# Gate products of a one-hot scatter: one full fp32 product against two fp32r products, with some of the one-hot columns on GpSimd

## The chip, the cores and the metric

The kernel runs on one core of one Trainium2 chip. The metric is the device time of one launch in microseconds (us). Three runs of the kernel before took 2625.31, 2624.11 and 2623.07 us, median 2624.11.

## What is computed

Two layers of a hybrid decoder run over 256 prompt tokens and 8 sample tokens. Each layer has three mixers with a common output projection, and then PEER, a product-key retrieval over 128 x 128 experts of one neuron each. The change is in PEER for the prompt tokens. Cut to what matters, the reference says:

```
q = (h @ wq).reshape(T, PEER_HEADS, 2, PEER_KDIM // 2)
s = einsum('thpc,hpkc->thpk', q, subkeys)
s_top, i_top = top_k(s, 16)                    # per head and side
cand = s_top[:, :, 0, :, None] + s_top[:, :, 1, None, :]
cs, ci = top_k(cand, 16)                       # 16 experts per head
g = softmax(cs)                                # their gates
act = gelu(einsum('td,thkd->thk', h, u[e]))
out = einsum('thk,thkd->td', g * act, v[e])
```

An expert is a pair (a, b) with number 128 a + b. A token uses 8 heads x 16 = 128 of the 16384 experts.

## The kernel before, in words

The kernel does not gather rows of u and v for the prompt tokens. It goes over all 16384 experts in 128 tiles of 128: tile j of `peer_u` is loaded, turned by TensorE (`turn_u`, L982), and multiplied with the normed activations of 256 tokens (`z_of`, L992). ScalarE's gelu of the product lands in G (L1266, L1267), which holds one number for each expert, token and tile. G is then multiplied with the gates, and a second stage of 128 tiles (`y_of`, L1038) multiplies it with `peer_v`.

**The gates** come as a dense 128 x 128 table for each token, made by one product: a one-hot matrix of a's (hotA: row = slot of the token, column = expert number a) times a matrix of b's whose one-hot entries carry the gate (hotB). Their product has for every pair the sum of its gates. The 256 tokens are taken in 64 groups of four (GG = 4). Group g is made in tile j = 64 + g, so this work lies in the second half of the first stage alone, in each of the two layers.

**One tile of the second half** on TensorE, in order: `z_of(j)`, 24 fp32r products with 256 moving columns (three for each of 8 pieces, since h and u are each split in a high fp32r part and the rest); `turn_u(j + 2)`, 8 transposes; `gates(g)`, 4 full fp32 products of 128 x 128 x 128 (L1004). Every full fp32 product is two instructions in the profile, each with its own weight load, so `gates` has 8 a tile and L1004 counts 1024 for 2 layers x 64 groups x 4 products.

`gates(g)` waits for three semaphores: hotA_ready (VectorE, L1824, all four tokens in one instruction of 512 columns), hotB_ready (VectorE, L1827, tokens 0 and 1, one instruction each) and hotC_ready (ScalarE, tokens 2 and 3: Abs of the distance to the index at L1250, then Relu with scale and bias at L1254). hotA and hotB have two buffers each, by g % 2, so the columns for group g + 1 can be written while group g is multiplied.

**The other engines in a tile.** VectorE, in order: multiply the rows of G that already have gates (L1851), the low parts of the turned u tile (`turned_low`, L1816), the one-hot columns (L1824, L1827), and `gate_rows` (L1837, L1839), which waits for the gate product and multiplies it into G. ScalarE: gelu, high parts of the turned tile (L1244), the copy of the rest of the gate product (L1292), its one-hot columns. GpSimd does nothing in this stage. Its queue stands at a wait for e_ready, then one for the last z product, and behind them are the indirect loads of expert rows for the sample tokens. SyncE's queue loads the tiles of u and v and copies state.

A granted clock (PEclk) of 1.00 is TensorE's level of 2.4 GHz, 0.50 that of 1.2 GHz.

## Time and profile before

| | |
|---|---|
| median of three runs | 2624.11 us |
| the profiled execution's own time | 2624.88 us |
| its span, first to last instruction | 2623.3 us |
| mean granted TensorE clock | 0.956 |
| PE busy | 2453.7 us, 94% |
| DVE busy | 1621.5 us, 62% |
| ACT busy | 1299.0 us, 50% |
| POOL busy | 105.6 us, 4% |

The engines are PE (TensorE's products), PEld (its weight loads, which overlap PE), DVE (VectorE), ACT (ScalarE), POOL (GpSimd) and SP (SyncE). Busy time is a union of intervals, so where instructions of one engine overlap in the pipeline, busy time is less than count x mean duration. The pace of a run of products is best read from the starts of the weight loads, since the ends of matmuls are modelled.

### The profile page before, as it was taken

The page shows a single profiled execution, that of the slowest core. Times are in us where ns is not written, and L with a number is a line of the kernel's source. Part 1 is how long each engine was busy: PE and PEld are TensorE (multiplying, and loading weights), DVE is VectorE, ACT ScalarE, POOL GpSimd, SP SyncE. Part 2 cuts the span into 40 slices and gives each one's busy share as a digit, 9 for nine tenths or more (in the row PEclk, how much of TensorE's full clock was granted, in tenths as well). Part 3 has the DMA queues.
Part 4 walks back from the last instruction along what each step waited for, and adds up shares of the span by engine and source line. Part 5 has one row for each costly group of instructions (what it writes and reads, how often), then busy time and mean ns, then how long its engine had stood idle before and what let it go on. Part 6 is the DMA issues. An engine that isn't in the chain of part 4 may idle for free.

```text
span 2623.3 us, 46433 instructions
## 1 busy us (share of the span) xinstructions
PE 2453.7 (94%) x17162; PEld 2100.0 (80%) x17162; DVE 1621.5 (62%) x3830; ACT 1299.0 (50%) x2860; POOL 105.6 (4%) x140
## 2 busy tenths in 40 slices
PE   6987899999999999999889878999999999999997
PEld 3564489999999988778645545799999999887785
DVE  2365247775677777767534641577756777776676
ACT  1342223545766666666413421245457666666664
POOL 2100010000000000000011000100000000000000
PEclk9997899999999999999988968999999999999998
DMA  7431226667555557666473312366665555676663
GB/s 231 147 127 66 81 99 224 241 234 252 192 208 191 209 196 242 219 196 194 127 240 130 116 65 81 114 233 244 246 234 196 199 207 195 204 238 221 196 193 128
DMA packets 143189, 482.43 MB, mean 184 GB/s; under 512 B 25282, under 2 KB 52224, under 8 KB 138862
## 3 DMA queue, kind: packets, MB, share of 16 engines
q1 hardware_dynamic: 132478, 439.11, 49.6%
q0 software_dynamic: 10496, 40.42, 4.4%
q8 instruction: 140, 2.29, 0.3%
q14 instruction: 75, 0.61, 0.1%
HBM read 476.20 MB, written 104.21 MB: 221 GB/s over the span
## 4 chain that ended last, share of the span: by engine, by line
PE 90%; DVE 5%; issue 1%; DMA 1%; ACT 1%; SPq 0%; POOL 0%; DVEq 0%; POOLq 0%; ACTq 0%
PE ps L992 28%; PE ps L1038 26%; PE ps L712 13%; PE ps L982 8%; PE ps L1004 4%; PE ps L703 4%; PE ps L721 1%; DMA region<-in_w_in 1%; PE ps L830 1%; PE ps L968 1%; PE ps L860 1%; PE ps L833 1%; PE ps L846 0%; DMA region<-in_cache_k_rope,pidx 0%; DVE big L1360 0%
## 5 line engine op out<-in xcount | busy, mean ns | idle before, releaser
L992 PE MATMUL ps<-parts_hw,parts_uv 128*128 128x256 f32 x6144 | 801.2, 287 | 9.1 <-DVE parts_uv L1816 9.1
L992 PEld LDWEIGHTS ps<-parts_hw,parts_uv 128*128 128x128 f32 x6144 | 754.8, 192 | 10.2 <-issue 10.0
L1038 PE MATMUL ps<-parts_uv,parts_hw 128*128 128x512 f32 x3072 | 705.5, 392 | 11.6 <-DVE parts_hw L1884 8.2
L1038 PEld LDWEIGHTS ps<-parts_uv,parts_hw 128*128 128x128 f32 x3072 | 579.4, 189 | 139.9 <-issue 15.4
L1880 DVE TENSOR_TENSOR parts_uv<-region,parts_uv 128x512 fp32r<-128x512 f32 x512 | 351.7, 691 | 196.1 <-ACT parts_uv L1303 195.8
L1303 ACT CAST parts_uv<-region 128x512 fp32r<-128x512 f32 x512 | 317.8, 622 | 248.7 <-PE ps L1038 247.5
L1816 DVE TENSOR_TENSOR parts_uv<-ps,parts_uv 128x512 fp32r<-128x512 f32 x512 | 329.5, 686 | 163.7 <-ACT parts_uv L1244 160.2
L1244 ACT CAST parts_uv<-ps 128x512 fp32r<-128x512 f32 x512 | 278.9, 599 | 1.5 <-PE ps L982 1.5
L1267 ACT ACTIVATE big<-ps 128x256 f32<-128x256 f32 (+26 forms) x256 | 129.7, 507 | 279.8 <-PE ps L992 279.8
L982 PE MATMUL ps<-ident,region 128*128 128x128 f32 x2048 | 265.5, 273 | 1.4 <-ACT big L1235 1.4
L712 PE MATMUL ps<-region 128*128 128x264 f32 (+3 forms) x832 | 234.1, 442 | 6.7 <-DMA region<-in_w_in 6.0
L982 PEld LDWEIGHTS ps<-ident,region 128*128 128x128 f32 x2048 | 230.0, 141 | 1.7 <-ACT big L1235 1.7
L712 PEld LDWEIGHTS ps<-region 128*128 128x128 f32 x832 | 159.1, 193 | 74.8 <-issue 34.7
L703 PE MATMUL ps<-ident,big 128*128 128x128 f32 (+2 forms) x518 | 102.8, 332 | 73.0 <-DVE big L1390 57.1
L1308 ACT CAST parts_hw<-big 128x256 fp32r<-128x256 f32 x256 | 168.7, 661 | 0.0
L1884 DVE TENSOR_TENSOR parts_hw<-big,parts_hw 128x256 fp32r<-128x256 f32 x256 | 157.8, 617 | 3.3 <-ACT parts_hw L1308 3.2
L703 PEld LDWEIGHTS ps<-ident,big 128*128 128x128 f32 (+2 forms) x518 | 72.4, 173 | 103.0 <-DVE big L1390 58.1
L1851 DVE TENSOR_TENSOR big<-big 128x4 f32<-128x4 f32 (+62 forms) x126 | 54.6, 434 | 155.1 <-ACT big L1267 155.1
L1004 PE MATMUL ps<-region 128*128 128x128 f32 x1024 | 135.2, 275 | 0.0
L1004 PEld LDWEIGHTS ps<-region 128*128 128x128 f32 x1024 | 124.5, 192 | 0.0
L1266 ACT ACTIVATE big<-ps 128x4 f32<-128x4 f32 (+62 forms) x126 | 34.9, 277 | 156.1 <-PE ps L992 156.1
L1254 ACT ACTIVATE region<-big,region 128x128 f32<-128x128 f32 x256 | 111.2, 483 | 0.0
(273 smaller groups left out, 1937.1 us busy)
## 6 DMA issues: line engine op xcount, KB each, us to landing
region<-in_peer_u SPq DMA_DIRECT2D x256, 512.0 KB, 3.9
region<-in_peer_v SPq DMA_DIRECT2D x256, 512.0 KB, 4.3
out<-in_state_win_k SPq DMA_DIRECT2D x16, 1536.0 KB, 8.9
out<-in_state_win_v SPq DMA_DIRECT2D x16, 1536.0 KB, 8.5
out<-in_state_win_k SPq DMA_DIRECT2D x16, 1534.5 KB, 9.1
out<-in_state_win_v SPq DMA_DIRECT2D x16, 1534.5 KB, 7.4
region<-in_peer_wq SPq DMA_DIRECT2D x8, 2048.0 KB, 8.2
region<-in_w_in SPq DMA_DIRECT2D x6, 1536.0 KB, 7.8
```

The lines of the kernel that those rows point to most:

```text
L703: mm = pe.transpose(o[0:cols, c0:c0 + rows], src, ident[0:rows, 0:rows])
L712: mm = pe.matmul(o[0:n_out, 0:cols], lhs, rhs, start=(i == 0), stop=(i == len(parts) - 1))
L982: mm = pe.transpose(ps[:, 2 * (j % 2) + half, 128 * i:128 * i + 128], rows_t[j % UN][:, 128 * c:128 * c + 128], ident[:, :])
L992: mm = pe.matmul(ps[:, 4 + j % 2, 0:SEQ], uT[j % 2][a][:, 128 * c:128 * c + 128], hp[b][:, c, :], start=(c == 0 and n == 0), stop=(c == KD ...
L1004: mm = pe.matmul(ps[:, 6 + g % 2, 128 * k:128 * k + 128], hotA[g % 2][:, k, :], hotB[g % 2][:, k, :], start=True, stop=True)
L1038: mm = pe.matmul(ps[:, 2 * half + t, :], wp[j % UN][a][:, 128 * t:128 * t + 128], vp[j % 2][b][:, 512 * half:512 * half + 512], start=(j = ...
L1244: act.copy(uT[j % 2][0][:, 512 * half:512 * half + 512], ps[:, 2 * (j % 2) + half, :]).then_inc(uT_high, 1)
L1303: act.copy(vp[j % 2][0][:, h], rows_t[j % UN][:, h]).then_inc(v_high, 1)
L1308: act.copy(wp[j % UN][0], G[:, j // JH, :, j % JH]).then_inc(w_high, 1)
L1816: dve.tensor_tensor(uT[j % 2][1][:, h], ps[:, 2 * (j % 2) + half, :], uT[j % 2][0][:, h], ALU.subtract).then_inc(uT_low, 1)
L1880: dve.tensor_tensor(vp[j % 2][1][:, h], rows_t[j % UN][:, h], vp[j % 2][0][:, h], ALU.subtract).then_inc(v_low, 1)
L1884: dve.tensor_tensor(wp[j % UN][1], G[:, j // JH, :, j % JH], wp[j % UN][0], ALU.subtract).then_inc(w_ready, 1)
```

## The change

- hotA and hotB leave their place in the region tile for a tile of their own, `hot_r`, of type fp32r. hotA keeps two buffers by group. hotB's index is now the part: hotB[0] high, hotB[1] low. It has one buffer for all groups.
- The gates of the 256 tokens are split once per layer, at j = 63: ScalarE writes the high part rounded to fp32r (a copy in the place of the negation that Relu needed), VectorE subtracts to get the rest.
- `gates` has two fp32r products for each token, hotA x hotB[0] and hotA x hotB[1], summed in PSUM, with 128 moving columns each.
- VectorE writes both parts of tokens 0 and 1, four instructions for two. GpSimd writes both parts of tokens 2 and 3, four instructions of the same kind. ScalarE's Abs and Relu go.
- With one buffer, the columns of group g + 1 wait for the product of group g. On VectorE they now come after `gate_rows(g)`.
- GpSimd's loop over the 64 groups stands ahead of the indirect loads in its queue.

The diff, cut to its core:

```diff
@@ -177,8 +177,6 @@
         wslot = [region[:, i * 4096:(i + 1) * 4096] for i in range(2)]
         rows_t = [region[:, 4096 + i * 1024:4096 + (i + 1) * 1024] for i in range(UN)]
-        hotA = [region[:, O_HT + i * 512:O_HT + (i + 1) * 512].rearrange("p (a b) -> p a b", a=GG) for i in range(2)]
-        hotB = [region[:, O_HT + 1024 + i * 512:O_HT + 1024 + (i + 1) * 512].rearrange("p (a b) -> p a b", a=GG) for i in range(2)]
         hB = region[:, O_HT:O_HT + 1024]
         gyS = region[0:NB, O_HT:O_HT + 2048].rearrange("p (g c) -> p g c", g=4)
@@ -186,12 +184,15 @@
 
 
         partA = sb("parts_uv", [P, 4 * 1024], F32R)
-        gap = sb("gap", [P, 4 * 1024 + KD * T])
+        gap = sb("gap", [P, 4 * 1024])
+        hot_r = sb("hot_r", [P, KD * T], F32R)
         partB = sb("parts_hw", [P, 4 * 1024], F32R)
         uT = [[partA[:, (2 * i + p) * 1024:(2 * i + p + 1) * 1024] for p in range(2)] for i in range(2)]
         vp = uT
         hp = [partB[:, i * KD * SEQ:(i + 1) * KD * SEQ].rearrange("p (k t) -> p k t", k=KD) for i in range(2)]
         wp = [[partB[:, (2 * i + p) * SEQ:(2 * i + p + 1) * SEQ] for p in range(2)] for i in range(UN)]
+        hotA = [hot_r[:, i * 512:(i + 1) * 512].rearrange("p (a b) -> p a b", a=GG) for i in range(2)]
+        hotB = [hot_r[:, 1024 + i * 512:1024 + (i + 1) * 512].rearrange("p (a b) -> p a b", a=GG) for i in range(2)]
         G = big[:, 0:BIG].rearrange("p (q t j) -> p q t j", q=2, j=JH)
         at = [0]
 
@@ -298,8 +299,7 @@
         rsel = cut(P)[0:TOPK]
         hsum = cut(2 * PH).rearrange("p (s h) -> p s h", s=2)
         tail = big[:, BIG:BIG + TAIL]
-        nw = tail[:, 0:SEQ]
-        dist = [tail[:, SEQ + i * P:SEQ + (i + 1) * P] for i in range(2)]
+        gate = [tail[:, i * SEQ:(i + 1) * SEQ] for i in range(2)]
         act_t = [tail[:, 528 + i * SEQ:528 + (i + 1) * SEQ] for i in range(2)]
         hS = tail[:, 1040:1104].rearrange("p (k b) -> p k b", k=KD)
 
@@ -372,8 +372,9 @@
         coef_ready = sem("sample_weights_ready")
         hotA_ready = sem("onehot_a_ready")
         hotB_ready = sem("onehot_b_ready")
-        dist_ready = sem("onehot_distance")
-        hotC_ready = sem("onehot_b_by_scalar")
+        gate_high = sem("gates_high")
+        gate_low = sem("gates_low")
+        hotC_ready = sem("onehot_b_by_gpsimd")
         g_prod = sem("gate_product")
         g_moved = sem("gate_moved")
         g_used = sem("gate_product_used")
@@ -674,6 +675,15 @@
                     pool.indirect_dma_start(gath[b % 2], None, A[name].rearrange("l e d -> (l e) d"), row).then_inc(done, 16)
 
                 pool.wait_ge(e_ready, 1)
+                pool.wait_ge(gate_low, 1)
+                for g in range(NGRP):
+                    if g:
+                        pool.wait_ge(g_prod, g)
+                    for k in range(2, GG):
+                        tk = slice(GG * g + k, GG * g + k + 1)
+                        for i in range(2):
+                            e = pool.tensor_scalar(hotB[i][:, k, :], iota[:, :], slotT[:, 1, tk], gate[i][:, tk], ALU.is_equal, ALU.mult)
+                    e.then_inc(hotC_ready, 1)
                 pool.wait_ge(z_prod, NK)
                 for b in range(NB):
                     if b >= 2:
@@ -1001,7 +1011,8 @@
                         pe.wait_ge(g_used, g - 1)
                         pe.wait_ge(g_moved, g - 1)
                     for k in range(GG):
-                        mm = pe.matmul(ps[:, 6 + g % 2, 128 * k:128 * k + 128], hotA[g % 2][:, k, :], hotB[g % 2][:, k, :], start=True, stop=True)
+                        for i in range(2):
+                            mm = pe.matmul(ps[:, 6 + g % 2, 128 * k:128 * k + 128], hotA[g % 2][:, k, :], hotB[i][:, k, :], start=(i == 0), stop=(i == 1))
                     mm.then_inc(g_prod, 1)
 
                 wait_moved(pe, "s", 1, 3)
@@ -1243,17 +1254,6 @@
                         act.wait_ge(turned, 2 * j + half + 1)
                         act.copy(uT[j % 2][0][:, 512 * half:512 * half + 512], ps[:, 2 * (j % 2) + half, :]).then_inc(uT_high, 1)
 
-                def onehots(g):
-                    if g >= 1:
-                        act.wait_ge(hotC_ready, g)
-                    for k in range(2):
-                        act.activation(dist[k], iota[:, :], ACT.Abs, bias=slotT[:, 1, GG * g + 2 + k:GG * g + 3 + k], scale=-1.0).then_inc(dist_ready, 1)
-                    for k in range(2):
-                        tk = slice(GG * g + 2 + k, GG * g + 3 + k)
-                        act.wait_ge(dist_ready, 2 * g + k + 2)
-                        e = act.activation(hotB[g % 2][:, 2 + k, :], dist[k], ACT.Relu, bias=slotT[:, 2, tk], scale=nw[:, tk])
-                    e.then_inc(hotC_ready, 1)
-
                 turned_high(0)
                 turned_high(1)
                 for j in range(NK):
@@ -1284,15 +1284,13 @@
                         act.copy(slotT[:, :, t0:t0 + m], o[:, 0:384].rearrange("p (s c) -> p s c", s=3)[:, :, 0:m]).then_inc(moved_a, 1)
                     if j == JH - 1:
                         wait_moved(act, "slot", 1)
-                        act.activation(nw, slotT[:, 2, 0:SEQ], ACT.Copy, scale=-1.0).then_inc(dist_ready, 1)
+                        act.copy(gate[0].bitcast(F32R), slotT[:, 2, 0:SEQ]).then_inc(gate_high, 1)
                     if j >= JH:
                         g = j - JH
                         act.wait_ge(g_prod, g + 1)
                         if g < NGRP - 1:
                             act.copy(G[:, 1, GG * g:GG * g + GG, g + 1:JH],
                                      ps[:, 6 + g % 2, :].rearrange("p (a b) -> p a b", a=GG)[:, :, JH + g + 1:NK]).then_inc(g_moved, 1)
-                    if JH - 1 <= j < NK - 1:
-                        onehots(j - JH + 1)
 
                 def v_parts(j):
                     act.wait_ge(row_ld[j % UN], 16 * (NK // UN + j // UN + 1))
@@ -1815,16 +1813,19 @@
                         dve.wait_ge(uT_high, 2 * j + half + 1)
                         dve.tensor_tensor(uT[j % 2][1][:, h], ps[:, 2 * (j % 2) + half, :], uT[j % 2][0][:, h], ALU.subtract).then_inc(uT_low, 1)
 
-                def onehots(g):
-                    if g == 0:
-                        wait_moved(dve, "slot", 1)
+                def onehots_a(g):
                     if g >= 2:
                         dve.wait_ge(g_prod, g - 1)
                     ta = slotT[:, 0, GG * g:GG * g + GG].unsqueeze(2).to_broadcast([P, GG, P])
                     dve.tensor_tensor(hotA[g % 2], iota[:, :].unsqueeze(1).to_broadcast([P, GG, P]), ta, ALU.is_equal).then_inc(hotA_ready, 1)
+
+                def onehots_b(g):
+                    if g:
+                        dve.wait_ge(g_prod, g)
                     for k in range(2):
                         tk = slice(GG * g + k, GG * g + k + 1)
-                        e = dve.tensor_scalar(hotB[g % 2][:, k, :], iota[:, :], slotT[:, 1, tk], slotT[:, 2, tk], ALU.is_equal, ALU.mult)
+                        for i in range(2):
+                            e = dve.tensor_scalar(hotB[i][:, k, :], iota[:, :], slotT[:, 1, tk], gate[i][:, tk], ALU.is_equal, ALU.mult)
                     e.then_inc(hotB_ready, 1)
 
                 def gate_rows(g):
@@ -1868,10 +1869,17 @@
                         step(dve.scalar_tensor_tensor(efl[:, :], pr[:, 0, :], float(NK), pr[:, 1, :], ALU.mult, ALU.add))
                         settle()
                         dve.tensor_scalar(eidx[:, :], efl[:, :], eoff[:, 0:1], None, ALU.add).then_inc(e_ready, 1)
+                    if j == JH - 1:
+                        wait_moved(dve, "slot", 1)
+                        dve.wait_ge(gate_high, 1)
+                        dve.tensor_tensor(gate[1], slotT[:, 2, 0:SEQ], gate[0], ALU.subtract).then_inc(gate_low, 1)
+                        dve.wait_ge(gate_low, 1)
                     if JH - 1 <= j < NK - 1:
-                        onehots(j - JH + 1)
+                        onehots_a(j - JH + 1)
                     if j >= JH:
                         gate_rows(j - JH)
+                    if JH - 1 <= j < NK - 1:
+                        onehots_b(j - JH + 1)
 
                 def v_low_part(j):
                     for half in range(2):
```

## Rows read from the trace of the kernel before

**Rows 1.** The page's chain that ended last, by line.

```profile
PE ps L992 28%; PE ps L1038 26%; PE ps L712 13%; PE ps L982 8%; PE ps L1004 4%; PE ps L703 4%; PE ps L721 1%; DMA region<-in_w_in 1%; PE ps L830 1%; PE ps L968 1%; PE ps L860 1%; PE ps L833 1%; PE ps L846 0%; DMA region<-in_cache_k_rope,pidx 0%; DVE big L1360 0%
```

**Rows 2.** Windows: first half, second half, value stage; busy us (instructions), PEclk, DMA share, GB/s.

```profile
400.00:640.00 240.00, 240.00 (x2039) 239.33 (x2038) 164.84 (x403) 106.12 (x201) 0.57 (x1) 0.99 0.69 242
642.00:930.00 288.00, 288.00 (x2489) 288.00 (x2488) 206.78 (x497) 197.04 (x563) 0.00 (x0) 1.00 0.57 198
940.00:1305.00 365.00, 357.87 (x1584) 291.99 (x1584) 257.11 (x415) 230.53 (x385) 13.81 (x14) 0.99 0.62 200
```

**Rows 3.** Timeline, one tile of the second half; start us, us, engine, line.

```profile
816.24 0.97 PEld L1004 LDWEIGHTS ps<-region 128*128 128x128 f32 x8
...
817.13 2.93 PEld L992 LDWEIGHTS ps<-parts_hw,parts_uv 128*128 128x128 f32 x24
...
817.44 0.25 ACT L1292 COPY big<-ps 128x104 f32<-128x104 f32 x1 [0.26 <-PE ps L1004]
...
817.94 0.68 DVE L1824 TENSOR_TENSOR region<-iota,region 128x512 f32<-128x512 f32 x1
818.18 0.87 ACT L1254 ACTIVATE region<-big,region 128x128 f32<-128x128 f32 x2
818.54 0.60 DVE L1827 TENSOR_SCALAR region<-iota,region 128x128 f32<-128x128 f32 x2
819.05 0.41 DVE L1837 TENSOR_TENSOR big<-big,ps 128x256 f32<-128x256 f32 x1
819.38 0.30 DVE L1839 TENSOR_TENSOR big<-big,ps 128x152 f32<-128x152 f32 x1
820.01 0.90 PEld L982 LDWEIGHTS ps<-ident,region 128*128 128x128 f32 x8
...
820.88 0.30 PEld L1004 LDWEIGHTS ps<-region 128*128 128x128 f32 x2
```

**Rows 4.** The page's groups: weight loads; busy us, mean ns of one.

```profile
L992 PEld LDWEIGHTS ps<-parts_hw,parts_uv 128*128 128x128 f32 x6144 | 754.8, 192 | 10.2 <-issue 10.0
...
L1004 PEld LDWEIGHTS ps<-region 128*128 128x128 f32 x1024 | 124.5, 192 | 0.0
```

**Rows 5.** The chain in order of time, value stage; start us, us, what.

```profile
950.32 127.85 PE ps L1038 x564
```

**Rows 6.** Timeline, weight loads of full fp32 products with 64 moving columns.

```profile
169.46 0.30 PEld L811 LDWEIGHTS ps<-big,region 128*128 128x128 f32 x2 [0.61 <-ACT region L1159]
169.68 0.30 PEld L812 LDWEIGHTS ps<-big,region 128*128 128x128 f32 x2
169.90 0.30 PEld L813 LDWEIGHTS ps<-big,region 128*128 128x128 f32 x2
```

**Rows 7.** Windows: the stretch around Rows 6.

```profile
169.20:170.30 1.10, 1.07 (x9) 0.84 (x9) 1.07 (x3) 1.10 (x4) 0.00 (x0) 1.00 0.00 0
```

**Rows 8.** Timeline, a late tile of the same half.

```profile
925.12 0.60 DVE L1827 TENSOR_SCALAR region<-iota,region 128x128 f32<-128x128 f32 x2
925.64 0.42 DVE L1837 TENSOR_TENSOR big<-big,ps 128x256 f32<-128x256 f32 x1
925.97 0.41 DVE L1839 TENSOR_TENSOR big<-big,ps 128x244 f32<-128x244 f32 x1
...
927.44 0.64 PEld L1004 LDWEIGHTS ps<-region 128*128 128x128 f32 x5
```

**Rows 9.** Line 1827 by its source view: duration ns min/median/max.

```profile
L1827 DVE TENSOR_SCALAR region<-iota,region x256: 334/342/365, 643.4 to 2237.4; 128x128 f32<-128x128 f32 x128
```

**Rows 10.** GpSimd's groups by line: busy us, mean ns of one.

```profile
L604 POOL MEMSET ones<- 128x128 f32 x1 | 0.2, 204 | 0.3 <-POOLq L1970 0.3
```

**Rows 11.** Waits of the second half: us in total, times, longest us.

```profile
ACT big L1266 <- PE ps L992: 75.4, 61, 1.3
```

**Rows 12.** Timeline, entry into the second half.

```profile
643.38 0.60 DVE L1827 TENSOR_SCALAR region<-iota,region 128x128 f32<-128x128 f32 x2
...
644.81 0.30 PEld L1004 LDWEIGHTS ps<-region 128*128 128x128 f32 x2
```

## The prediction, made before the changed kernel was run

> **What bounds the kernel.** I read the chain first. L992, the products of the first PEER stage, hold 28% of the span, L1038 26%, the transposes L982 8% and the gate products L1004 4% [rows 1]. L1004 is thus on the path with its whole busy time. The stage table says how: in the second half of the first stage TensorE is busy 288.00 us of 288 at clock 1.00, VectorE 206.78, ScalarE 197.04, GpSimd 0 [rows 2]. Nothing there waits for VectorE or ScalarE; the other way round, ScalarE's gelu waits for the z product 61 times, 75.4 us in all [rows 11]. So any nanosecond on TensorE in a tile is paid 128 times (64 tiles in each of two layers), and anything on another engine costs nothing until it passes the slack that I work out below.
>
> The timeline of one tile gives the paces. Weight loads of the gate products start at 816.24, those of the next z at 817.13: 0.89 us for 8 instructions, 111 ns each. The z loads run to 820.01, 2.88 us for 24, 120.0 ns each. Eight transposes take 0.87 us, and the next gate products start at 820.88, 4.64 us after the last [rows 3].
>
> **TensorE's part.** The change keeps the number of instructions: 4 full fp32 products of two instructions each become 8 fp32r products of one. What counts is the spacing of an fp32r product with 128 moving columns, which this trace does not have; all its fp32r products have 256 or 512. The naive reading is that work halves. Two rows speak against it.
>
> First, streaming need not be the limit. L811 to L813 are full fp32 products with a 128-column weight and only 64 moving columns. Their loads start 0.22 us apart for two instructions, 110 ns each, at clock 1.00 [rows 6, 7]. That is the spacing of the gate products too, though these stream twice the columns. So in both a load of 128 weight columns takes the time. Second, the fp32r load is no shorter than the fp32 one: 192 ns mean on L992 and 192 on L1004 [rows 4]. Every fp32r product has its own load too, 6144 loads on L992 though two of three share their weights, so I count no load as saved.
>
> Then where between the ends? Below: streaming alone. The value stage has 564 products of 512 columns in 127.85 us, 226.7 ns each [rows 5]; against 120.0 for 256 columns that is 106.7 ns for 256 columns, 0.417 a column, and 120.0 - 53.3 = 66.7 ns for 128 columns. Above: each fp32r product as dear as the full fp32 product that it takes the place of, 222 ns. Between them lie 111 (the load, at fp32's spacing) and 120.0 (the load, at fp32r's spacing on L992). I take 120.0, because that row is nearest: same type, same load, and the 13 ns over 106.7 that fp32r shows at 512 columns as at 256 look like a cost of each instruction and not of its columns. The term is 1024 x (120.0 - 111) = **+9.2 us**.
>
> The Trainium skill, page "TensorE: Matmul & The Clock Gate", section "Back-to-back issue gap", states some 81 ns for load and product in a sustained stream with 128 moving columns. By that the term would be 1024 x (81 - 111) = -31 us; no row here shows that pace, and the 110 ns of [rows 6] speak against it.
>
> **VectorE's part.** Two more column writes a tile. The pair at L1827 takes 819.05 - 818.54 = 0.51 us, 0.255 each in a stream and 0.34 alone [rows 3, 9], so +0.51 us a tile on an engine busy 206.78 / 288 x 4.64 = 3.33 us of 4.64. It is hidden, if the chain holds: in the new order hotA ends at 818.54; gate_rows, 819.05 to 819.68 before, takes 0.63 to 819.17; four writes, 3 x 0.255 + 0.34 = 1.11, end at 820.28. The next gate products are due at 820.88: slack 0.60 us. In a late tile gate_rows grows: 925.12 + (926.38 - 925.64) + 1.11 = 926.97 against 927.44, slack 0.47 [rows 8]. Some 0.53 on the mean, and 0.07 more where the tile is longer by 8 x 9 ns. Cost nothing; the cover is z of the next tile, and without it each 0.1 us is worth 12.8 us. That these writes wait for the product of group g adds nothing on VectorE, since gate_rows ahead of them waits for the same.
>
> The fp32r output of hotA and hotB: between nothing and a few per cent of 0.5 us; I take nothing.
>
> **ScalarE's part.** Abs and Relu go, the Relu pair alone 0.87 us from 818.18 [rows 3]. ScalarE only waits more for TensorE: no gain.
>
> **GpSimd's part.** Four column writes a tile, from the release of group g's product (817.44, when ScalarE's copy starts) to 820.88: 3.44 us, so 0.86 for each is the limit. The trace has no such instruction on GpSimd. Below stands its memset of 128 x 128, 204 ns [rows 10]; above, twice VectorE's own 342, some 0.68 us, as an estimate. Both fit alone: cost nothing. Its queue: the loop now stands ahead of the indirect loads, which wait for the last z product anyway, and the loop ends a tile before that: nothing.
>
> **Once per layer.** Before, the first columns were ready at 643.38 + 0.60 = 643.98, and TensorE came at 644.81, slack 0.83 [rows 12]. New on VectorE: a subtraction of 256 columns (0.41, as L1837's), its store and wait (0.1, my estimate) and two writes (0.51), 1.02: 0.2 us late, twice, **+0.4 us**. GpSimd starts at 643.3 and ends 0.82 to 2.7 later, so this could be 2 us more.
>
> **Sum.** 9.2 + 0.4 = 9.6 us onto the profiled execution's 2624.88: **2634.5 us**. That execution stands 0.77 above the median of the runs, well within their own spread.
>
> **Rivals.**
> 1. *Loads keep fp32's spacing.* The 13 ns belong to fp32r's streaming, which is hidden at 128 columns, and 111 ns stay. For: L811 and L1004 agree with each other within 1 ns whatever they stream. Against: both are fp32. Time 2624.88 + 0.4 = 2625.3.
> 2. *Streaming is the limit after all (faster).* 66.7 ns: -1024 x 44.3 = -45.4 us, 2579.9. For: "two fp32r passes for four" is the plain count of work, and a load's record of 192 ns may hold latency that overlaps, as it does on L992, where loads start every 120. Against: the 110 ns of [rows 6]. VectorE would just follow: the tile shrinks by 0.35 us, under its slack. The Trainium skill's 81 ns of the page named above is of this kind, and gives 2594.
> 3. *A short fp32r product is as dear as a full fp32 one.* 222 ns: +1024 x 111 = +113.7, 2739. Nothing in the trace excludes it; nothing in it shows such a jump between 512 and 256 columns either.
> 4. *GpSimd ahead of hotA (slower).* GpSimd's four writes start at 817.44, while VectorE still has 0.50 us of low parts to do. If hotA then has to stand behind all four, it starts 4p - 0.50 late, p being one GpSimd write; after a slack of 0.60 the stall is 4p - 1.10 us a tile, from p = 0.28 on. At p = 0.41, twice the memset, 0.54 x 128 = 69 us: 2704. At 0.68 it would be 207. If only one write stands ahead, it decides from p = 0.60 alone. The Trainium skill, page "SBUF — State Buffer", section "Who interferes with whom", gives a reason for such an order: a VectorE instruction with two SBUF inputs, as hotA (index and slots), and a GpSimd one that reads SBUF block each other for a whole instruction. No run here has shown it, GpSimd being idle in this stage.
>
> **How the numbers follow.** Forecast 0.34, rival 1 0.23, rival 2 with all values between 66.7 and 105 ns 0.20, rival 3 0.12, rival 4 0.11. The range goes from 2576, just under rival 2, to 2668, which holds the smaller half of rival 4; out are rival 3 and the rest of rival 4, 0.18. A measurement can tell 0.2%, some 5 us, from no change. Faster by over that: rival 2, 0.20. Within: rival 1, 0.23. Slower: the forecast with its +9.6 us and rivals 3 and 4, 0.57.
>
> **What would show it.** The gate products' weight loads at 120 ns, 0.96 us for 8, and a tile of 4.70 us; 1024 instructions as before; no waits of TensorE on hotB or hotC beyond the first of each layer; hotA starting as the low parts end. A spacing near 111 makes rival 1 right, near 67 rival 2, near 222 rival 3. If TensorE waits in each tile for the columns, rival 4 is right, and hotA's start and p say how. I am wrong altogether if the time moves outside this half stage.

## The result and the profile after

The changed kernel takes 2656.74 us, median of four runs (2654.54 to 2661.28), against 2624.11 before: a ratio of 1.0126, 95% interval 1.0109 to 1.0144. It is 32.6 us, or 1.3%, slower. The forecast was 2634.5, its range 2576 to 2668.

The groups of the page after that answer to [rows 4], [rows 9] and the idle GpSimd of [rows 2]; columns as there (busy us, mean ns of one, idle before and its releaser):

```profile
L685 POOL TENSOR_SCALAR hot_r<-iota,region,big 128x128 fp32r<-128x128 f32 x512 | 444.7, 879 | 593.7 <-DVE big L1875 414.3
...
L1015 PE MATMUL ps<-hot_r 128*128 128x128 f32 x1024 | 138.3, 278 | 17.3 <-issue 11.5
L1828 DVE TENSOR_SCALAR hot_r<-iota,region,big 128x128 fp32r<-128x128 f32 x512 | 152.8, 368 | 0.0
...
L1015 PEld LDWEIGHTS ps<-hot_r 128*128 128x128 f32 x1024 | 123.9, 191 | 34.0 <-issue 29.8
```

The same stretch as in [rows 2] by windows, a little shorter so that the entry is left out (busy us of PE, PEld, DVE, ACT, POOL, then PEclk, DMA share, GB/s):

```profile
645.00:930.00 285.00, 282.84 (x2364) 277.14 (x2364) 231.56 (x590) 106.06 (x296) 200.34 (x239) 0.99 0.55 193
```

GpSimd, idle before, is busy 200 of 285 us, and one of its writes takes 0.88 us on the mean. TensorE has only 2364 instructions in 285 us, where before it had 2489 in 288: the same work at a slower tile. Its gate products still number 1024, and the mean of their loads is 191 ns against 192.

One tile by the timeline, the answer to [rows 3]:

```profile
815.09 0.97 PEld L1015 LDWEIGHTS ps<-hot_r 128*128 128x128 f32 x8
...
815.98 2.94 PEld L1002 LDWEIGHTS ps<-parts_hw,parts_uv 128*128 128x128 f32 x24
...
816.30 3.43 POOL L685 TENSOR_SCALAR hot_r<-iota,region,big 128x128 fp32r<-128x128 f32 x4 [1.39 <-PE ps L1015]
816.72 0.68 DVE L1820 TENSOR_TENSOR hot_r<-iota,region 128x512 fp32r<-128x512 f32 x1
...
817.86 1.17 DVE L1828 TENSOR_SCALAR hot_r<-iota,region,big 128x128 fp32r<-128x128 f32 x4
818.86 0.90 PEld L992 LDWEIGHTS ps<-ident,region 128*128 128x128 f32 x8
...
819.90 0.97 PEld L1015 LDWEIGHTS ps<-hot_r 128*128 128x128 f32 x8
```

The eight gate loads take 815.98 - 815.09 = 0.89 us, 111 ns each, the old pace to the nanosecond. Then the loop shows. The product's release lets GpSimd start at 816.30, its four writes end at 819.73, and the next gate loads start at 819.90. So a tile is 0.89 + 0.32 to GpSimd's start + 3.43 + 0.17 = 4.81 us against TensorE's own 4.64. VectorE's four writes end at 819.03, well before.

Four writes at 0.79 us, what one takes by itself (a row below has it), would be 3.16 us, and the loop 4.54 us, under TensorE's own tile. It is over it because GpSimd's writes grow beside VectorE. In the first layer hotA (L1820) mostly starts 0.3 to 0.5 us after GpSimd's first write. That first write takes 0.79 us, the second, which runs beside hotA, 0.93 by the median, and the third, beside VectorE's column writes (L1828), 0.88.

In the second layer, and there only from about the 27th group on, the tile is longer still:

```profile
2123.61 0.97 PEld L1015 LDWEIGHTS ps<-hot_r 128*128 128x128 f32 x8 [0.45 <-issue]
...
2124.50 2.94 PEld L1002 LDWEIGHTS ps<-parts_hw,parts_uv 128*128 128x128 f32 x24
...
2124.82 0.68 DVE L1820 TENSOR_TENSOR hot_r<-iota,region 128x512 fp32r<-128x512 f32 x1
2124.82 3.78 POOL L685 TENSOR_SCALAR hot_r<-iota,region,big 128x128 fp32r<-128x128 f32 x4 [1.40 <-PE ps L1015]
...
2127.39 0.90 PEld L992 LDWEIGHTS ps<-ident,region 128*128 128x128 f32 x8
...
2128.79 0.97 PEld L1015 LDWEIGHTS ps<-hot_r 128*128 128x128 f32 x8 [0.50 <-issue]
...
2129.95 0.68 DVE L1820 TENSOR_TENSOR hot_r<-iota,region 128x512 fp32r<-128x512 f32 x1
2130.00 1.29 POOL L685 TENSOR_SCALAR hot_r<-iota,region,big 128x128 fp32r<-128x128 f32 x1 [1.39 <-PE ps L1015]
```

Here hotA (L1820) starts just before GpSimd's first write or with it. That write takes 1.29 us. In the tiles of 4.7 to 4.8 us, where GpSimd starts first, a first write takes 0.79:

```profile
811.59 0.79 POOL L685 TENSOR_SCALAR hot_r<-iota,region,big 128x128 fp32r<-128x128 f32 x1 [1.40 <-PE ps L1015]
```

With the longer first write the four take 3.78, and the tile is 0.89 + 0.32 + 3.78 + 0.19 = 5.18 us. The source views give the spread, GpSimd's write first (ns min/median/max):

```profile
L685 POOL TENSOR_SCALAR hot_r<-iota,region,big x512: 780/828/1348, 643.0 to 2271.5; 128x128 fp32r<-128x128 f32 x171
```

```profile
L1820 DVE TENSOR_TENSOR hot_r<-iota,region x128: 670/682/834, 642.8 to 2267.9; 128x512 fp32r<-128x512 f32 x128
L1828 DVE TENSOR_SCALAR hot_r<-iota,region,big x512: 329/343/454, 643.4 to 2270.9; 128x128 fp32r<-128x128 f32 x171
```

hotA's median of 682 ns is that of before, 681; its longest, 834, is near the entry. VectorE's column writes have a median of 343 ns against 342, but some are slowed as well: the longest is 454 against 365 [rows 9], the mean 368 against 342.

And the entry of the stage, the answer to [rows 12]:

```profile
642.34 0.41 DVE L1875 TENSOR_TENSOR big<-region,big 128x256 f32<-128x256 f32 x1
...
642.96 3.77 POOL L685 TENSOR_SCALAR hot_r<-iota,region,big 128x128 fp32r<-128x128 f32 x4 [207.15 <-DVE big L1875]
...
646.84 0.97 PEld L1015 LDWEIGHTS ps<-hot_r 128*128 128x128 f32 x8 [2.45 <-issue]
...
647.73 4.43 PEld L1002 LDWEIGHTS ps<-parts_hw,parts_uv 128*128 128x128 f32 x24
```

VectorE's subtraction ends at 642.75, GpSimd's first four writes at 646.73, and TensorE waits until 646.84 where before it began at 644.81. The z products after that wait take 4.43 us instead of 2.93. The granted clock of their stretch is 0.60 on the mean, so most of it ran at the level of 1.2 GHz:

```profile
647.80:652.10 4.30, 4.30 (x26) 4.30 (x25) 1.70 (x6) 0.37 (x1) 3.18 (x4) 0.60 0.01 2
```

**Where the time went, by the starts of the gate loads.** From a layer's first z product to its first gate load: 249.89 and 249.83 us after, 247.46 and 247.48 before, +4.8 together. From the first gate load to the last: 301.70 and 315.02 against 290.15 twice, +36.4; of it 1.5 a layer are the first tile at the lower clock, and about 2 a layer the last two intervals, which have no transposes between the products: 3.75 and 3.77 before, 4.84 and 4.58 now in the first layer, 5.20 and 4.58 in the second. The sum is 41 us. The span grew by 33.6 only, because the stretch between the two layers' PEER stages took 394.6 us in this execution and 401.4 in that of before.

Some of this difference comes with the change. Of the ten kernels that were traced, the two whose columns are full fp32 in the region tile (before and experiment 2) have 401.4 and 401.5 us there, seven of the eight with `hot_r` have 394.4 to 398.1, and one of them (experiment 3) has 404.6. At one place all eight agree: the first products with the next layer's w_in start 27.0 to 29.1 us after the last product of the value stage, in before and experiment 2 31.9 and 32.7. TensorE waits for the load of w_in less long there, in before and after:

```profile
1331.31 2.42 PE L712 MATMUL ps<-region 128*128 128x416 f32 x3 [6.04 <-DMA region<-in_w_in]
1340.91 2.42 PE L722 MATMUL ps<-region 128*128 128x416 f32 x3 [1.98 <-DMA region<-in_w_in]
```

Why it waits less was not tried. The medians of experiments 1, 5, 6 and 7 below also lie 7 to 10 us lower than the starts of their gate loads would have them, that of experiment 3 lies 5 lower, and that of experiment 2, which has no `hot_r`, 4, so a part of this may be chance. The change costs some 41 us in the half stage, and the total hides some of it.

### The profile page after: what moved, and what is told of

The parts are those of the page before. It is cut to its first block, busy times and chain, and to the rows that moved or that the text cites. A ratio compares the mean times of both kernels' runs of the same rounds, so it can differ in the third digit from the quotient of the medians.

```text
span 2656.9 us, 46699 instructions
## 1 busy us (share of the span) xinstructions
PE 2473.7 (93%) x17162; PEld 2104.6 (79%) x17162; DVE 1700.1 (64%) x4088; ACT 1124.9 (42%) x2348; POOL 547.5 (21%) x652
## 4 chain that ended last, share of the span: by engine, by line
PE 89%; DVE 6%; issue 2%; SPq 1%; DMA 1%; ACT 1%; POOL 1%; DVEq 0%; POOLq 0%; ACTq 0%
PE ps L1002 28%; PE ps L1049 26%; PE ps L722 12%; PE ps L992 8%; PE ps L1015 5%; PE ps L713 4%; PE ps L731 1%; PE ps L840 1%; PE ps L978 1%; PE ps L870 1%; PE ps L843 1%; PE ps L856 0%; DMA region<-in_cache_k_rope,pidx 0%; DVE big L1358 0%; DVE big L1479 0%
## 5 line engine op out<-in xcount | busy, mean ns | idle before, releaser
L685 POOL TENSOR_SCALAR hot_r<-iota,region,big 128x128 fp32r<-128x128 f32 x512 | 444.7, 879 | 593.7 <-DVE big L1875 414.3
L992 PE MATMUL ps<-ident,region 128*128 128x128 f32 x2048 | 265.3, 273 | 1.4 <-ACT big L1246 1.4
L992 PEld LDWEIGHTS ps<-ident,region 128*128 128x128 f32 x2048 | 229.9, 141 | 1.7 <-ACT big L1246 1.7
L722 PEld LDWEIGHTS ps<-region 128*128 128x128 f32 x832 | 158.9, 193 | 71.8 <-issue 30.4
L1015 PE MATMUL ps<-hot_r 128*128 128x128 f32 x1024 | 138.3, 278 | 17.3 <-issue 11.5
L1828 DVE TENSOR_SCALAR hot_r<-iota,region,big 128x128 fp32r<-128x128 f32 x512 | 152.8, 368 | 0.0
L1015 PEld LDWEIGHTS ps<-hot_r 128*128 128x128 f32 x1024 | 123.9, 191 | 34.0 <-issue 29.8
```

The costliest lines, as they stand in the source:

```text
L685: e = pool.tensor_scalar(hotB[i][:, k, :], iota[:, :], slotT[:, 1, tk], gate[i][:, tk], ALU.is_equal, ALU.mult)
L722: mm = pe.matmul(o[0:n_out, 0:cols], lhs, rhs, start=(i == 0), stop=(i == len(parts) - 1))
L992: mm = pe.transpose(ps[:, 2 * (j % 2) + half, 128 * i:128 * i + 128], rows_t[j % UN][:, 128 * c:128 * c + 128], ident[:, :])
L1015: mm = pe.matmul(ps[:, 6 + g % 2, 128 * k:128 * k + 128], hotA[g % 2][:, k, :], hotB[i][:, k, :], start=(i == 0), stop=(i == 1))
```

## The experiments

Each ratio compares with the kernel before, measured again beside the experiments; its medians were 2625.88 (experiments 1 to 4) and 2627.58 (5 to 8).

The theory after reading the traces: a tile is now a loop through GpSimd, since hotB has one buffer and its writes cannot start before the product of the group ahead is done. The rivals: the fp32r products themselves (my forecast), VectorE's longer chain, or a mere sharing of something between GpSimd and VectorE.

**1. Two buffers for GpSimd's columns.**

```diff
-                    if g:
-                        pool.wait_ge(g_prod, g)
+                    if g >= 2:
+                        pool.wait_ge(g_prod, g - 1)
...
-                            e = pool.tensor_scalar(hotB[i][:, k, :], iota[:, :], slotT[:, 1, tk], gate[i][:, tk], ALU.is_equal, ALU.mult)
+                            e = pool.tensor_scalar(hotB(g, i, k), iota[:, :], slotT[:, 1, tk], gate[i][:, tk], ALU.is_equal, ALU.mult)
...
-                    if g >= 2:
-                        dve.wait_ge(g_prod, g - 1)
+                    if g:
+                        dve.wait_ge(g_prod, g)
```

`hotB(g, i, k)` gives for tokens 2 and 3 the buffer of g % 2, for tokens 0 and 1 the only one. To make room, hotA has one buffer instead of two, so VectorE writes it only after the product of the group ahead (the last two pairs of lines). Experiments 4, 6 and 8 share this.

> The change as it is, but GpSimd's columns (tokens 2 and 3, both parts) have two buffers by g % 2, so that GpSimd starts on group g + 1 once the product of group g - 1 is done, a tile earlier; hotA has one buffer instead of two, to make room. Theory (the tile is the loop of the gate product 0.89, its release, GpSimd's four writes 3.3 to 3.75 and the wait's end, 4.7 to 5.15 us): the loop is cut, GpSimd's four writes fit in a tile of TensorE's own 4.64 us, the tiles return to 4.64, and 2656.7 falls to 2626 to 2634 (what is left is the entry of each layer, where TensorE waits 2.4 us and then runs some tiles' worth of work at the lower clock). Rival A (the fp32r products with 128 moving columns or VectorE's longer chain are what costs): the tile stays at 4.77 or more, 2645 to 2657.

Measured: 2626.61 us (11 runs), ratio 1.0003, interval 0.9992 to 1.0014. One tile by the timeline, and a stretch by windows:

```profile
801.66 0.97 PEld L1019 LDWEIGHTS ps<-hot_r 128*128 128x128 f32 x8
...
802.55 2.93 PEld L1006 LDWEIGHTS ps<-parts_hw,parts_uv 128*128 128x128 f32 x24
...
802.87 3.49 POOL L689 TENSOR_SCALAR hot_r<-iota,region,big 128x128 fp32r<-128x128 f32 x4 [1.15 <-PE ps L1019]
803.35 0.68 DVE L1824 TENSOR_TENSOR hot_r<-iota,region 128x512 fp32r<-128x512 f32 x1
...
805.42 0.68 PEld L996 LDWEIGHTS ps<-ident,region 128*128 128x128 f32 x6
```

```profile
700.00:900.00 200.00, 200.00 (x1729) 200.00 (x1729) 170.39 (x432) 77.30 (x217) 150.42 (x172) 1.00 0.57 200
```

GpSimd's four writes still take 3.49 us, but they are those of the group after next. TensorE is busy all of the time again, and nearly all of the 32 us is gone. The intervals between gate loads are 4.63 to 4.65 us in both layers, but for the first, 6.14, and the last two, 4.2 and 3.76. This kernel still has the fp32r products and VectorE's longer chain. So neither lengthens a tile, and the loop through GpSimd is the cause. The entry still has its wait of 2.45 us. By the starts of the gate loads this kernel still takes some 9 us more than the kernel before: 4.9 in the wait at the entries, 3.0 in the first tiles at the lower clock and 1 in the last two intervals. That the medians differ by only 0.7 us fits the shorter time outside the half stage named above.

**2. GpSimd alone, in the kernel before.** ScalarE's Abs and Relu go, GpSimd writes tokens 2 and 3 in full fp32, two instructions a tile with two buffers; products and VectorE stay.

```diff
...
+                for g in range(NGRP):
+                    if g >= 2:
+                        pool.wait_ge(g_prod, g - 1)
+                    for k in range(2, GG):
+                        tk = slice(GG * g + k, GG * g + k + 1)
+                        e = pool.tensor_scalar(hotB[g % 2][:, k, :], iota[:, :], slotT[:, 1, tk], slotT[:, 2, tk], ALU.is_equal, ALU.mult)
...
-                    if JH - 1 <= j < NK - 1:
-                        onehots(j - JH + 1)
```

> The kernel before, with one part of the change: GpSimd writes the one-hot columns of tokens 2 and 3 (full fp32, one instruction each, two buffers as before) in place of ScalarE's Abs and Relu. The products stay full fp32. Theory: two writes of 0.83 us with a tile of room are hidden, 4.64 us a tile, 2622 to 2627. Rival (GpSimd's mere presence slows VectorE through what they share, or ScalarE's relief is worth something): over 2630, or below 2620.

Measured: 2622.17 us (10 runs), ratio 0.9987, interval 0.9973 to 1.0002: no difference. The timeline:

```profile
800.80 1.87 POOL L683 TENSOR_SCALAR region<-iota,region 128x128 f32<-128x128 f32 x2 [2.77 <-PE ps L1012]
801.23 0.68 DVE L1816 TENSOR_TENSOR region<-iota,region 128x512 f32<-128x512 f32 x1
...
805.43 0.80 POOL L683 TENSOR_SCALAR region<-iota,region 128x128 f32<-128x128 f32 x1 [2.77 <-PE ps L1012]
```

VectorE's hotA keeps its 0.68 us beside GpSimd. The two GpSimd writes take 1.87 and not 2 x 0.80; the second runs beside hotA. So GpSimd's writes do grow beside VectorE, and it costs nothing while GpSimd has room. The intervals between gate loads are those of the kernel before, 4.63 us. Taking Abs and Relu off ScalarE gave nothing that can be measured.

**3. hotA earlier on VectorE,** with everything else as in the change.

```diff
+                    if JH <= j < NK - 1:
+                        onehots_a(j - JH + 1)
                     if j + 2 < NK:
                         turned_low(j + 2)
...
-                    if JH - 1 <= j < NK - 1:
-                        onehots_a(j - JH + 1)
+                    if j == JH - 1:
+                        onehots_a(0)
```

> The change as it is, with one instruction moved on VectorE: hotA of the next group is written right after the multiply (before the low parts of the turned tile) instead of after them, so that it no longer runs beside GpSimd's first write. Theory (hotA, two inputs from SBUF, and a GpSimd write hold each other up, which is why GpSimd's four take 3.3 to 3.4 us where hotA starts 0.3 to 0.45 us after them and 3.75 where it starts with them, against 4 x 0.79): the four writes take 3.2 us in every tile, the loop comes to 4.6 and the tile to TensorE's 4.64 to 4.70, 2630 to 2638. Rival (GpSimd's pace is its own, or other VectorE instructions do the same): bursts of 3.4 to 3.75 remain and the time stays at 2650 to 2660.

Measured: 2634.31 us (9 runs), ratio 1.0036, interval 1.0022 to 1.0050. The timeline:

```profile
799.97 0.68 DVE L1820 TENSOR_TENSOR hot_r<-iota,region 128x512 fp32r<-128x512 f32 x1
...
800.57 1.28 DVE L1814 TENSOR_TENSOR parts_uv<-ps,parts_uv 128x512 fp32r<-128x512 f32 x2
...
800.80 3.25 POOL L685 TENSOR_SCALAR hot_r<-iota,region,big 128x128 fp32r<-128x128 f32 x4 [1.40 <-PE ps L1015]
...
804.23 0.97 PEld L1015 LDWEIGHTS ps<-hot_r 128*128 128x128 f32 x8
```

hotA now runs ahead of GpSimd's writes, these take 3.25 us, and the loop, 0.89 + 0.32 + 3.25 + 0.17 = 4.63, is just as long as TensorE's tile. The gate loads are 4.58 to 4.82 us apart in both layers, all but the first of each, 6.15 and 6.12. One instruction in another place took 22 of the 32 us by the medians; from the first gate load to the last the two layers took 28.6 us less than in the change. So two things had to come together: the loop, which experiment 1 opens, and the growth of GpSimd's writes beside hotA, which this one takes away. What is left are the entry and the last two tiles. It does not say which of hotA's properties makes GpSimd wait; only that its place does.

**4. Weights of 64 columns,** on top of experiment 1. Rows 64 to 127 of each gate table are left out.

```diff
-                            mm = pe.matmul(ps[:, 6 + g % 2, 128 * k:128 * k + 128], hotA[g % 2][:, k, :], hotB(g, i, k), start=(i == 0), stop=(i == 1))
+                            mm = pe.matmul(ps[0:64, 6 + g % 2, 128 * k:128 * k + 128], hotA[g % 2][:, k, 0:64], hotB(g, i, k), start=(i == 0), stop=(i == 1))
```

> As e1_gpsimd_two_buffers, but the gate products take only the first 64 columns of hotA as weights, so that rows 64 to 127 of each gate table are not computed (left out). The moving columns stay 128. Theory (the spacing of 111 ns is the load of 128 weight columns): the spacing falls to 60 to 80 ns and the tile from 4.64 to 4.3 or 4.4 us. Rival (111 ns is the streaming or a fixed cost of a short fp32r product): it stays at 105 to 111 ns.

Measured: 2582.46 us, one run. The weight loads by the timeline:

```profile
801.60 0.61 PEld L1019 LDWEIGHTS ps<-hot_r 128*64 128x64 f32 x8
...
802.13 2.94 PEld L1006 LDWEIGHTS ps<-parts_hw,parts_uv 128*128 128x128 f32 x24
```

Eight loads in 0.53 us, 66 ns each, with the same 128 moving columns; the tile is 4.29 us. So the spacing of 111 ns goes with the number of weight columns and is their load. And 66 is what I had worked out as the pure streaming pace of rival 2, 66.7; that streaming is the limit with half the load agrees with it, but was not shown by itself.

**5. The gates split three tiles earlier,** with everything else as in the change (`j == SPLIT`, 60, for `j == JH - 1` at the split on ScalarE and VectorE).

> The change as it is, but the gates are split at j = 60 instead of 63, so that GpSimd writes the columns of group 0 three tiles earlier. Theory (each layer's entry costs 2.45 us of waiting for GpSimd's first four writes plus 1.5 us for the next z at the lower clock that follows the wait): some 3.5 to 4 us a layer go, 7 to 8 in all, and 2656.7 falls to about 2649; the tiles stay at 4.77 to 5.15 us. Rival (the entry is hidden in the loop that follows, which has to wait for GpSimd anyway): under 3 us.

Measured: 2651.41 us (4 runs), ratio 1.0080, interval 1.0051 to 1.0109. The weight loads at the entry:

```profile
645.33 0.90 PEld L993 LDWEIGHTS ps<-ident,region 128*128 128x128 f32 x8
646.19 0.97 PEld L1016 LDWEIGHTS ps<-hot_r 128*128 128x128 f32 x8
647.08 2.93 PEld L1003 LDWEIGHTS ps<-parts_hw,parts_uv 128*128 128x128 f32 x24
```

TensorE goes from the transposes to the gate products without a wait, and the z products that follow have 2.93 us again. So the entry's mechanism is shown by the trace, and its size too: from the first z product to the last gate load, both layers together, this kernel took 7.9 us less than the change, against 7 to 8 expected. The medians cannot show it: the runs lie between 2636.3 and 2655.4, and the interval meets that of the change. The tiles are 4.64 to 4.97 in the first layer and 5.0 to 5.2 in the second from the same group on.

**6. Experiments 1 and 5 together.**

> e1_gpsimd_two_buffers with the split at j = 60. Theory: no wait on GpSimd is left, and the products cost what the full fp32 ones did: the tile 4.64 us, entry as before, so 2619 to 2626, no measurable gain over the kernel before. Rival (ScalarE's relief or the shorter accumulation is worth something): below 2617.

Measured: 2620.82 us (12 runs), ratio 0.9984, interval 0.9973 to 0.9996. A stretch by windows:

```profile
700.00:900.00 200.00, 200.00 (x1729) 200.00 (x1729) 170.50 (x433) 76.49 (x216) 151.23 (x174) 1.00 0.58 200
```

With no wait on GpSimd left, the products cost what they did: the intervals between gate loads are 4.63 us, and from the first to the last a layer takes 290.6 us against 290.15 before. The gain of 0 to 0.3% in the median is therefore not theirs; in the trace it lies between the layers, 394.4 us against 401.4.

**7. The parts in bf16.** The same eight products and eight column writes a tile, hotA and both parts of hotB as bf16, which take half the room, so all have two buffers; the split is at j = 60, as in experiment 5. The gate's high part is the gate rounded to bf16, the low part the rest rounded to bf16; what lies below both is left out.

```diff
-        hot_r = sb("hot_r", [P, KD * T], F32R)
+        hot_r = sb("hot_r", [P, 2 * KD * T], BF16)
...
-                        act.copy(gate[0].bitcast(F32R), slotT[:, 2, 0:SEQ]).then_inc(gate_high, 1)
+                        act.copy(gate_b, slotT[:, 2, 0:SEQ]).then_inc(gate_high, 1)
+                        act.wait_ge(gate_high, 1)
+                        act.copy(gate[0], gate_b).then_inc(gate_high, 1)
```

> The products' type alone changed against e6: hotA and both parts of hotB are bf16 (the gate as a bf16 high part and the rest rounded to bf16, about 16 bits of mantissa kept; the rest below is left out), all with two buffers since they take half the room; split at j = 60. Same number of products, 8 of 128 moving columns a tile, and of column writes. Theory (the spacing of 111 ns was the load of 128 4-byte weight columns, since it fell to 66 with 64 of them): a 2-byte load is shorter, the spacing 55 to 80 ns, the tile 4.2 to 4.4 us, 2570 to 2595 in all. The Trainium skill, page 'TensorE: Matmul & The Clock Gate', section 'Back-to-back issue gap', gives 81 ns, which would be 4.40 us a tile. Rival (a load of 128 columns takes its 107 ns whatever the type): 4.6 us a tile, 2617 to 2626. Second rival: VectorE or GpSimd become the bound at the shorter tile (GpSimd 3.3 to 3.75 us a tile, VectorE 3.9): waits of TensorE on the columns.

Measured: 2572.79 us (5 runs), ratio 0.9796, interval 0.9782 to 0.9811: 2.0% faster than the kernel before (1.9 to 2.2 by the interval) and 84 us below the change. The timeline, the source view of the gate products (ns min/median/max), and the stretch by windows:

```profile
799.78 3.75 POOL L688 TENSOR_SCALAR hot_r<-iota,region,big 128x128 bf16<-128x128 f32 x4 [0.49 <-PE ps L1018]
...
800.66 0.70 DVE L1825 TENSOR_TENSOR hot_r<-iota,region 128x512 bf16<-128x512 f32 x1
...
803.20 0.54 PEld L1018 LDWEIGHTS ps<-hot_r 128*128 128x128 bf16 x8
...
803.70 1.61 PEld L1005 LDWEIGHTS ps<-parts_hw,parts_uv 128*128 128x128 f32 x13
```

```profile
L1018 PEld LDWEIGHTS ps<-hot_r x1024: 95/98/99, 642.1 to 2185.4; 128*128 128x128 bf16 x171
L1018 PE MATMUL ps<-hot_r x1024: 216/219/230, 642.2 to 2185.4; 128*128 128x128 bf16 x171
```

```profile
645.00:900.00 255.00, 255.00 (x2407) 254.22 (x2407) 237.43 (x602) 101.95 (x300) 219.20 (x241) 1.00 0.63 218
```

The spacing is (803.70 - 803.20) / 8 = 62 ns, and the load's record falls from 192 to 98 ns. The tile is 4.24 us, 0.39 shorter. From the first gate load to the last the two layers take 47.6 us less than before, of the 55 between the medians. TensorE is busy all the time. But VectorE is busy 237 of 255 us and GpSimd 219, so there is little room for more.

The Trainium skill, page "TensorE: Matmul & The Clock Gate", section "Weight-path perf modes", says that the fast weight load is on for 128 weights where the input type is not FP32. The two load records, 98 ns for bf16 and 192 for fp32r, agree with it, with fp32r counted as FP32. The 81 ns that the Trainium skill's same page, section "Back-to-back issue gap", has for a load and product of 128 moving columns is neither type's here, 62 and 111 ns.

**8. Both parts as 256 moving columns,** on top of experiment 1. The sum of the parts is left out, and two of four tokens' tables are overwritten.

```diff
-                        for i in range(2):
-                            mm = pe.matmul(ps[:, 6 + g % 2, 128 * k:128 * k + 128], hotA[g % 2][:, k, :], hotB(g, i, k), start=(i == 0), stop=(i == 1))
+                        both = hotV[:, :, k, :] if k < 2 else hotP[g % 2][:, :, k - 2, :]
+                        mm = pe.matmul(ps[:, 6 + g % 2, 256 * (k % 2):256 * (k % 2) + 256], hotA[g % 2][:, k, :], both, start=True, stop=True)
```

> As e1_gpsimd_two_buffers, but the two parts of a token's columns stand side by side as 256 moving columns of one product, 4 products a tile instead of 8; their two results are not added, and two of four tokens' tables are overwritten (left out: the sum of the parts, and so the right gates). Theory (one load of 128 columns each, and fp32r's fixed 13 ns over 106.7 of streaming as on the z products): 120 ns each, 0.48 us in place of 0.89, tile 4.2 to 4.3 us. Rival (an fp32r product here has another floor, such as its operands' place): over 150 ns each.

Measured: 2582.44 us, one run. The weight loads:

```profile
802.63 0.54 PEld L1019 LDWEIGHTS ps<-hot_r 128*128 128x128 f32 x4
803.10 2.22 PEld L1006 LDWEIGHTS ps<-parts_hw,parts_uv 128*128 128x128 f32 x18
```

0.47 us for four, 118 ns each: a product with 256 moving columns costs 7 ns more than one with 128. The tile is 4.22 us. What adding the two results would cost was not tried.

## Why the prediction was right and wrong

- **The outcome.** Slower was forecast, and 2656.7 lies inside the range. That is luck. The size was off, 9.6 us forecast and 32.6 measured, and so were the reasons: the term that I forecast is absent, and GpSimd's writes, which I set to nothing in a tile, make nearly all of the loss. By my own signs the case is rival 4's, since TensorE waits in each tile for the columns. Its sum does not fit either: with p = 0.79 its stall of 4p - 1.10 would be 2.06 us a tile. The measured one is 0.14 us on the mean in the first layer and about 0.5 in the late part of the second.
- **TensorE's part failed in its choice.** "The load, at fp32r's spacing on L992", 120.0 ns, +9.2 us: the spacing is 111, as in rival 1. That the load and not the streaming limits was right, as was the reading of [rows 6] against the naive count; experiment 4 shows it. What failed was adding fp32r's 13 ns over 106.7 to a product that its load limits. The 13 ns do not show at 128 columns. They do show where streaming would be the limit: 66 ns in experiment 4 against 53.3 for the columns alone, and 118 in experiment 8 against 106.7. So I read them as a part of the streaming, which the load hides.
- **GpSimd's part failed, and this is 33 of the 41 us by the gate loads.** "Both fit alone: cost nothing" rested on bounds of 0.20 and 0.68 us for a write. Alone it takes 0.78 to 0.80, beside hotA up to 1.35. The limit of 0.86 that I set was nearly right: 3.44 us less 0.06 and 0.17 for release and wait leave 0.80 each. So by itself even the real write would just have fitted. The step that failed is that it is never by itself: its second or first write runs beside hotA, the four take 3.24 to 3.80 us instead of 3.16, and the loop passes the tile. The memset, which reads nothing, was the wrong neighbour, and a factor of two over VectorE too small an upper bound; the factor is 0.79 / 0.34 = 2.3.
- **Rival 4 had the place and missed the direction.** It had GpSimd and hotA holding each other up, with VectorE as the one that waits. VectorE hardly does: hotA's median is 682 ns after and 681 before, and its column writes' mean is 368 against 342. GpSimd's write is what grows, from 0.79 to 1.29 us, and it is on the loop. The Trainium skill, page "SBUF — State Buffer", section "Who interferes with whom", says that a VectorE instruction with two SBUF inputs and a GpSimd one that reads SBUF block each other for a whole instruction. The first write's extra 0.50 us agrees in kind. But VectorE is not held up where GpSimd starts first: in experiment 1 hotA starts 0.48 us after GpSimd's first write and takes its 0.68 us all the same. No experiment here took hotA's second input away.
- **VectorE's part held.** The slack of about half a microsecond covered its two more writes: in the tile shown they end at 819.03, 0.87 us before the late gate loads. Their fp32r output costs nothing, as taken: the medians are 682 ns against 681 for hotA and 343 against 342 for a column write.
- **ScalarE's part held:** no gain from Abs and Relu, by experiment 2.
- **Once per layer** I had 0.4 us for both layers and named 2 as possible. It was about 4 a layer: 2.4 of waiting and 1.5 of the next z at the lower clock. The second half, a wait that also slows what follows, was in no term.
- **"I am wrong altogether if the time moves outside this half stage."** It moved there too, the other way: 41 us more by the gate loads and 32.6 in the median. The prediction had no term for it. TensorE's shorter wait for w_in, 1.98 us in place of 6.04, is a part of it, and its cause is open.

It stays open, too, why the second layer falls into the 5.1 us tile at the same group in two kernels (the change and experiment 5) and the first layer does not. As the rows read, it then holds itself: GpSimd ends later, the product comes later, and hotA, whose start hangs on the low parts, is again there when the product is released. The step is one interval of 4.99 us, after which hotA starts 0.11 us behind GpSimd's first write instead of 0.45. What tips it was not tried.

## What to carry to other kernels

Cost a short product by its weight load: with 128 columns of weights of 4 bytes and 128 moving columns, splitting one full fp32 product into two fp32r products saved nothing (111 ns each before and after), and going to 2-byte parts saved 44% of its time (62 ns). When a buffer is dropped to make room, write down the loop that it closes, product to write to product, with each release in it, and compare it with the tile; the engine in that loop was busy only 70% of the time. An idle engine's price for an operation has to be measured before it goes into such a loop, and measured beside what will run next to it.

## What the runs showed of the hardware that was not expected

- A GpSimd write of 128 x 128 with two per-partition scalars takes 0.78 to 0.80 us by itself and 1.29 where VectorE's hotA starts with it; VectorE's own takes 0.34. hotA itself keeps its 0.68.
- The place of one VectorE instruction of 0.68 us against GpSimd's writes was worth 22 us of the median, with VectorE busy 81% and GpSimd 70% of the stage.
- A wait of 2.4 us of TensorE was followed by z products of 4.43 us instead of 2.93, so the wait cost 1.5 us more than its length.
- The stretch between the two PEER stages was 394.4 to 404.6 us in ten traces, one of each kernel, and shorter in seven of the eight kernels with `hot_r` than in the other two. The kernel before varied by 15 us over 26 runs. So an effect of a few us in the tiles has to be read from intervals between loads and not from the total.
